# A decoder layer with an expert FFN: the first tile's output projection in three split passes

## The chip, the core and the metric

The kernel runs on one core of a Trainium2 chip. A core has five engines, each with its own queue that runs in order: TensorE (matrix products, PE in the rows), VectorE (DVE), ScalarE (ACT), GpSimd (POOL) and SyncE (SP), and 16 DMA engines. They wait for each other through semaphores only. The metric is the device time of one execution in microseconds, from the first instruction to the end; lower is better.

## What is computed

The reference is one hybrid decoder layer on 256 tokens of width 1024, in float32. The part that matters here is the mixer's output projection, `o @ w_out` of 1024 by 1024:

```python
def hybrid_mixer(h, w_in, b_forget, rel_bias, g_moba_out, g_fox_out, w_out):
    ...
    o_a = moba_attention(hd(qm, N_HEADS_MOBA), hd(km, N_HEADS_MOBA), hd(vm, N_HEADS_MOBA), rel_bias)
    o_b = forgetting_attention(hd(qf, N_HEADS_FOX), hd(kf, N_HEADS_FOX), hd(vf, N_HEADS_FOX),
                               fl + b_forget)
    o = jnp.concatenate([rmsnorm(o_a.reshape(B, S, MOBA_WIDTH), g_moba_out),
                         rmsnorm(o_b.reshape(B, S, FOX_WIDTH), g_fox_out)], axis=-1)
    return o @ w_out
...
    x = x + hybrid_mixer(...)
    x = x + memory_cross_attention(rmsnorm(x), rmsnorm(mem), ...)
    x = x + peer_ffn(rmsnorm(x), ...)     # per token 8 heads x 16 experts: rows of expert_down and expert_up
```

After the mixer come the cross-attention to 256 memory tokens and the expert FFN, which for each token fetches 128 rows of two expert tables.

## The kernel before

The 256 tokens are two tiles of 128 (tile 0 and tile 1). Everything up to the expert FFN is written as one list of steps, `main`, by hand: a step is a tuple such as `("S", t, i)`, `("PT", t, i)`, `("O", t, i)` (scores, transposed probabilities and values of head i of tile t) or `("wout", t, b, part)` (a quarter, two of the eight 128-row chunks, of block b of the output projection). TensorE, VectorE and ScalarE each walk the same list, and each does its own share of a step, so the place of a step in the list is its place in three queues. On VectorE and ScalarE a step in quarters stands where its last quarter stands.

The input projections and the memory's keys and values are products of split numbers: each float32 operand is split into a high part, rounded to the short format float32r, and a low part, the rest; high x high, high x low and low x high are added up in PSUM (`split_product`). The high part of a weight half is a ScalarE cast into `SPARE` (step `high`, L736), the low part a VectorE subtraction in place (step `low`, L976). The output projection is in plain float32 (`product`, L1374).

The attention of tile 0 is woven with the memory's values: eight rounds, p = 0 to 7, of one pair of heads and three or four quarters. After round 4 the first eight heads are normalised and squared (`o_out`, L1044; `o_root`, L667 and L680), after round 7 the other eight. `o_scale` (L1052) multiplies by the root's inverse, `oT` transposes one half on TensorE and VectorE writes it, times the gain, into `HT[0]` (`gained`, L926). Then the projection of tile 0 is woven into the attention of tile 1, tile 1's projection stands behind tile 0's cross-attention, and tile 0's first expert numbers are found by VectorE (`first_head`). GpSimd then issues one indirect DMA for each of 2 x 128 sets of 128 expert rows (L644), VectorE takes dot products of what lands (L1274), ScalarE makes a diagonal of weights and TensorE adds the rows up (L1634).

SyncE's queue issues the weight loads in a written order; each waits until the block that held the slot has been used (`load_block`). `w_out` lies in slots 0 and 1 for both tiles.

## Time and profile before

| | |
|---|---|
| median of 3 runs | 877.69 us (876.02 to 877.87) |
| the profiled execution, its own time | 878.16 us |
| its span, first to last instruction | 876.4 us |
| TensorE busy | 783.6 us, 89% |
| VectorE busy | 558.0 us, 64% |
| ScalarE busy | 437.9 us, 50% |
| GpSimd busy | 249.2 us, 28% |
| DMA | 316.80 MB, mean 362 GB/s |
| mean granted TensorE clock | 0.983 |

The busy shares are means over stages with different limits: up to some 235 us the layer's dense part runs, behind it the expert rows stream in. Clocks and times in the trace are those of the one profiled execution.

### The profile page before, as it was taken

The numbers are of one execution on the slowest core, as the hardware profiler recorded it, in microseconds if no ns is written. First come the engines' busy times: TensorE is split into PE (matmuls) and PEld (weight loads), VectorE is DVE, ScalarE is ACT, GpSimd is POOL, SyncE is SP. The second block draws the span as 40 slices with busy tenths as digits, with TensorE's granted clock in tenths as the row PEclk, the third lists the DMA queues.
The fourth block names the chain that finished last, engine by engine and source line by source line (L and its number), as shares of the span: only waits on it lengthen the run. The fifth ranks groups of instructions, "written<-read, shape, count | busy, mean of one in ns | idle before, by whom it ended". The sixth has DMA issues, their size and how long they took to land.

```text
span 876.4 us, 9609 instructions
## 1 busy us (share of the span) xinstructions
PE 783.6 (89%) x3144; PEld 445.7 (51%) x3144; DVE 558.0 (64%) x1374; ACT 437.9 (50%) x1105; POOL 249.2 (28%) x277
## 2 busy tenths in 40 slices
PE   8999999999999999888898997979787878888776
PEld 8999996895456455444343542544232322323222
DVE  5556443133888767777677658787666766666445
ACT  6447465342264554776545345545455454545344
POOL 1000000000343433434433441533333333343331
PEclk9999999999999999999999999989999999999999
DMA  9956931253899999999999999999999999999995
GB/s 352 417 149 166 424 122 82 72 217 144 318 423 420 402 423 420 421 422 421 421 421 422 420 421 403 418 423 421 420 421 423 421 424 421 423 421 422 421 422 238
DMA packets 44959, 316.80 MB, mean 362 GB/s; under 512 B 5075, under 2 KB 7156, under 8 KB 9972
## 3 DMA queue, kind: packets, MB, share of 16 engines
q0 software_dynamic: 37296, 268.98, 74.1%
q1 hardware_dynamic: 6588, 45.72, 13.2%
q10 hardware_dynamic: 1032, 1.57, 1.3%
q8 instruction: 22, 0.36, 0.2%
q14 instruction: 21, 0.17, 0.0%
HBM read 313.63 MB, written 2.62 MB: 361 GB/s over the span
## 4 chain that ended last, share of the span: by engine, by line
PE 43%; DMA 38%; DVE 8%; ACT 7%; issue 3%; SPq 0%; POOL 0%; POOLq 0%; DVEq 0%; ACTq 0%
DMA weights<-in_expert_rows,expert_idx 21%; PE y L1634 10%; DMA qkvb<-in_expert_rows,expert_idx 8%; PE v_bank L1634 8%; DMA mem_k<-in_expert_rows,expert_idx 7%; PE v_bank L1381 5%; PE v_bank L1374 4%; PE h_psum L1374 4%; PE h_psum L1381 3%; PE a_bank L1381 3%; PE a_bank L1374 2%; DVE weights L1274 2%; DMA spare_row<-in_expert_rows,expert_idx 1%; ACT diag L838 1%; ACT L829 1%
## 5 line engine op out<-in xcount | busy, mean ns | idle before, releaser
L829 ACT ACTIVATE gelu<-dots,stat 128x1 f32<-128x1 f32 x256 | 75.1, 294 | 291.4 <-DVE dots L1274 290.9
L644 POOL DMA_INDIRECT weights<-in_expert_rows,expert_idx x153 | 144.8, 947 | 252.1 <-PE y L1634 106.1
L1634 PE MATMUL v_bank<-weights,diag 128*128 128x512 f32 x316 | 157.9, 634 | 34.6 <-ACT diag L838 34.6
L1634 PE MATMUL y<-weights,diag 128*128 128x512 f32 x296 | 139.1, 606 | 13.8 <-ACT diag L838 13.8
L1274 DVE CUSTOM_DVE_ANT_0 weights<-a_bank,weights 128x1024 f32<-128x1024 f32 x79 | 96.7, 1224 | 63.9 <-DMA weights<-in_expert_rows,expert_idx 63.8
L1634 PEld LDWEIGHTS v_bank<-weights,diag 128*128 128x128 f32 x316 | 57.7, 197 | 130.6 <-ACT diag L838 79.3
L1274 DVE CUSTOM_DVE_ANT_0 weights<-h_psum,weights 128x1024 f32<-128x1024 f32 x74 | 90.5, 1223 | 45.9 <-DMA weights<-in_expert_rows,expert_idx 45.5
L838 ACT ACTIVATE diag<-ident,wgt 128x128 f32<-128x128 f32 x255 | 102.4, 401 | 8.3
L1634 PEld LDWEIGHTS y<-weights,diag 128*128 128x128 f32 x296 | 54.2, 192 | 81.2 <-issue 50.7
L644 POOL DMA_INDIRECT qkvb<-in_expert_rows,expert_idx x61 | 58.2, 954 | 107.7 <-PE v_bank L1634 44.4
L833 ACT ACTIVATE wgt<-gelu,gates 128x1 f32<-128x1 f32 x256 | 75.4, 294 | 8.3
L1634 PE MATMUL v_bank<-qkvb,diag 128*128 128x512 f32 x116 | 56.5, 611 | 10.2 <-ACT diag L838 10.2
L1634 PE MATMUL y<-qkvb,diag 128*128 128x512 f32 x128 | 59.9, 600 | 6.1 <-ACT diag L838 6.1
L976 DVE TENSOR_TENSOR weights_r<-weights,spare_r 128x2048 fp32r<-128x2048 f32 x18 | 41.3, 2292 | 30.2 <-ACT spare_r L736 30.2
L627 POOL DMA_INDIRECT gfin<-in_expert_rows,last_idx x1 | 1.1, 1102 | 198.2 <-PE y L1515 198.2
L1274 DVE CUSTOM_DVE_ANT_0 qkvb<-a_bank,qkvb 128x1024 f32<-128x1024 f32 x30 | 36.7, 1224 | 25.6 <-DMA qkvb<-in_expert_rows,expert_idx 25.5
L1274 DVE CUSTOM_DVE_ANT_0 qkvb<-h_psum,qkvb 128x1024 f32<-128x1024 f32 x32 | 39.1, 1223 | 17.3 <-DMA qkvb<-in_expert_rows,expert_idx 17.1
L736 ACT CAST spare_r<-weights 128x2048 fp32r<-128x2048 f32 x18 | 34.2, 1900 | 27.0 <-PE v_bank L1381 17.5
L1634 PEld LDWEIGHTS v_bank<-qkvb,diag 128*128 128x128 f32 x116 | 20.2, 189 | 44.9 <-ACT diag L838 28.9
L1634 PEld LDWEIGHTS y<-qkvb,diag 128*128 128x128 f32 x128 | 23.0, 190 | 34.9 <-issue 21.5
L644 POOL DMA_INDIRECT spare_row<-in_expert_rows,expert_idx x30 | 28.4, 946 | 39.8 <-PE y L1634 19.4
L1381 PE MATMUL v_bank<-scaled_gffn_r,spare_r 128*128 128x256 f32 x128 | 37.3, 291 | 1.2 <-DVE weights_r L962 1.2
(305 smaller groups left out, 1354.9 us busy)
## 6 DMA issues: line engine op xcount, KB each, us to landing
weights<-in_w_in SPq DMA_DIRECT2D x4, 2048.0 KB, 23.2
weights<-in_w_xk SPq DMA_DIRECT2D x2, 2048.0 KB, 13.8
weights<-in_w_xv SPq DMA_DIRECT2D x2, 2048.0 KB, 15.3
weights<-in_w_out SPq DMA_DIRECT2D x2, 2048.0 KB, 18.3
weights<-in_w_xq SPq DMA_DIRECT2D x2, 2048.0 KB, 7.9
weights<-in_w_xo SPq DMA_DIRECT2D x2, 2048.0 KB, 10.0
weights<-in_expert_rows,expert_idx POOLq DMA_INDIRECT x153, 15.1
weights<-in_w_in SPq DMA_DIRECT2D x2, 1024.0 KB, 12.2
```

What stands on the lines that cost most here:

```text
L627: pool.indirect_dma_start(gfin, None, half_rows, bass.IndirectOffsetOnAxis(ap=last_idx[:, 0:1], axis=0))\
L644: pool.indirect_dma_start(ROWS[buffer(n)], None, expert_rows, bass.IndirectOffsetOnAxis(ap=IDX[:, H % 3, k:k + 1], axis=0))\
L736: act.copy(WH_r[t % 2], half_block(t, W)).then_inc(high_ready, 1)
L829: nc.scalar.activation(gel[:, i:i + 1], dots[:, dot_of(n):dot_of(n) + 1], ACT.Gelu, scale=rms("root_p", n // SPT)).then_inc(gelu_done, 1)
L833: nc.scalar.activation(wgt[:, i:i + 1], gel[:, i:i + 1], ACT.Copy, scale=GATE[:, H % 3, k:k + 1])\
L838: nc.scalar.activation(diag[:, i, :], ident[:, :], ACT.Copy, scale=wgt[:, i:i + 1])\
L976: nc.vector.tensor_tensor(half_block(t, W_r), half_block(t, W), WH_r[t % 2].bitcast(f32), ALU.subtract).then_inc(low_ready, 1)
L1274: nc.vector.tensor_tensor_reduce(out=rows, in0=HP[n // SPT][:, :], in1=rows, scale=1.0, scalar=0.0, op0=ALU.mult, op1=ALU.add, accum_out=d ...
L1374: ins = nc.tensor.matmul(bank[:, lo:lo + n], lhs(k), rhs(k), start=(k == 0), stop=(k == chunks - 1))
L1381: ins = nc.tensor.matmul(bank[:, lo:lo + n], a(k), b(k), start=(begins and k == 0 and p == 0), stop=(ends and k == KC - 1 and p == 2))
L1634: ins = nc.tensor.matmul(YP[t][:, b * BLK:(b + 1) * BLK], diag[:, i, :], ROWS[r][:, D + b * BLK:D + (b + 1) * BLK], start=False, stop=last)
```

## The change

The projection of tile 0 becomes a split product in three passes. Its weights are split in eight pieces of two chunks by one block of 512 columns (`out_split(n)`): `out_high` on ScalarE casts a piece into one of four pages of 1024 columns (the second half of `spare_row`, `gfin`, the second page of `SG`, and `HTpage[1]`), `out_low` on VectorE subtracts in place in the weight slot. Pages are used twice; the second use waits until TensorE has used the first (`out_used`). The evacuation of `oT` of tile 0 writes a high part (`OH_r`, one instruction) and a low part (`OL_r`, four instructions). Since the low parts overwrite `w_out`, and tile 1 still projects in plain float32, SyncE loads both blocks a second time; the load of the gains `gffn` moves behind that, its wait is dropped, and the loads of `w_xq` come before both.

```diff
+    out_parts = [(b, 2 * half + c) for half in range(2) for b in range(2) for c in range(2)]
+
+    def out_split(n):
+        return [("out_high", n, 0), ("out_low", n, 0)]
...
-        main += {4: [("o_out", 0, 0), ("o_root", 0, 0), ("o_scale", 0, 0)],
-                 6: [("oT", 0, 0)]}.get(p, [])
+        main += {4: [("o_out", 0, 0), ("o_root", 0, 0), ("o_scale", 0, 0)] + out_split(0), 5: out_split(1),
+                 6: [("oT", 0, 0)] + out_split(2), 7: out_split(3)}.get(p, [])
     main += late + [("o_out", 0, 1), ("o_root", 0, 1)]
...
-    main += wout[0][:2] + pair("S", 1, 0) + wout[1][:2] + [("o_scale", 0, 1), ("oT", 0, 1)]
-    main += whole_pair(1, 0, wout[0][2:3]) + wout[0][3:] + whole_pair(1, 1, wout[1][2:3]) + wout[1][3:]
+    main += wout[0][:2] + pair("S", 1, 0) + [("o_scale", 0, 1)] + out_split(4) + wout[1][:2] + [("oT", 0, 1)] + out_split(5)
+    main += pair("PT", 1, 0) + pair("S", 1, 1) + out_split(6) + wout[0][2:3] + pair("O", 1, 0) + wout[0][3:] + out_split(7)
+    main += whole_pair(1, 1, wout[1][2:3]) + wout[1][3:]
...
-            sp.wait_ge(*full(("wina", 5, 1)))
-            sp.dma_start(gffn[:, :], A["norm_ffn"][0:1, :].broadcast_to([P, D])).then_inc(ld_gffn, 16)
             load_block("w_xq", 0)
             load_block("w_xq", 1)
+
+
+            for b in range(2):
+                sp.wait_ge(*full(("wout", 0, b)))
+                sp.dma_start(W[:, SLOT[("w_out", b)], :], A["w_out"][b]).then_inc(w_full[SLOT[("w_out", b)]], 16)
+            sp.dma_start(gffn[:, :], A["norm_ffn"][0:1, :].broadcast_to([P, D])).then_inc(ld_gffn, 16)
...
+                elif name == "out_high":
+
+                    b = out_parts[t][0]
+                    act.wait_ge(w_full[SLOT[("w_out", b)]], 16 * NTH[("w_out", b)])
+                    if t >= 4:
+                        act.wait_ge(out_used, t - 3)
+                    elif t >= 2:
+                        act.wait_ge(*full(("wina", 5, 1)))
+                    act.copy(out_pages[t % 4], out_block(t, W)).then_inc(out_high, 1)
...
+                elif name == "out_low":
+                    dve.wait_ge(out_high, t + 1)
+                    nc.vector.tensor_tensor(out_block(t, W_r), out_block(t, W), out_pages[t % 4].bitcast(f32),
+                                            ALU.subtract).then_inc(out_low, 1)
+                elif name == "oT" and t == 0:
+                    src = job(key)
+                    gain = gcol[:, 8 + 4 * i:12 + 4 * i].unsqueeze(2).broadcast_to([P, 4, P])
+                    nc.vector.tensor_tensor(OH_r[:, 4 * i:4 * i + 4, :], src[:, :].rearrange("p (c x) -> p c x", c=4),
+                                            gain, ALU.mult).then_inc(oh_ready, 1)
+                    dve.wait_ge(oh_ready, i + 1)
+                    for c in range(4):
+                        k = 4 * i + c
+                        ins = nc.vector.scalar_tensor_tensor(out=OL_r[:, k, :], in0=src[:, c * P:(c + 1) * P],
+                                                             scalar=gcol[:, 8 + k:9 + k], in1=OH_r[:, k, :].bitcast(f32),
+                                                             op0=ALU.mult, op1=ALU.subtract)
+                    ins.then_inc(v_free, 1)
...
+                    if t == 0:
+                        n = out_parts.index((i, part))
+                        w_low, w_high = out_block(n, W_r), out_pages[n % 4]
+                        if part % 2 == 0:
+                            pe.wait_ge(*freed(("oT", t, part // 2)))
+                        pe.wait_ge(out_low, n + 1)
+                        ins = split_product(bank, 0, BLK, lambda k: OH_r[:, k, :], lambda k: OL_r[:, k, :],
+                                            lambda k: w_high[:, k % 2, :], lambda k: w_low[:, k % 2, :],
+                                            range(2 * part, 2 * part + 2))
+                        if part < 2:
+                            ins.then_inc(out_used, 1)
```

ScalarE's queue from the root of tile 0's first half to the copy of round 6's transposes stood like this before (`stat` is the root, `mem_v` the memory's values, `spare_row` the probabilities and their transposes, `spare_r` the high parts):

```order
L680 ACTIVATE stat<-stat,eps 128x1 [waits sum_done]
L707 ACTIVATE mem_v<-h_psum,stat 128x256 [waits rows_root,m_full]
L707 ACTIVATE mem_v<-h_psum,stat 128x256
L767 COPY spare_row<-a_bank 128x128 [waits a_full] x2
L762 ACT_TABLE_LOAD [waits a_full]
L762 ACTIVATE spare_row,row_sum<-s_sb,neg_max 128x128 [waits v_free]
L762 ACTIVATE spare_row,row_sum<-s_sb,neg_max 128x128 [waits a_full,v_free]
L736 CAST spare_r<-weights 128x2048 [waits m_full,w_full4]
L767 COPY spare_row<-a_bank 128x128 [waits a_full] x2
```

Here the memory's values follow the root at once. ScalarE's queue at the same place now, with the lines of the changed file:

```order
L699 ACTIVATE stat<-stat,eps 128x1 [waits sum_done]
L764 CAST spare_row_r<-weights 128x1024 [waits w_full0]
L726 ACTIVATE mem_v<-h_psum,stat 128x256 [waits rows_root,m_full]
L726 ACTIVATE mem_v<-h_psum,stat 128x256
L795 COPY spare_row<-a_bank 128x128 [waits a_full] x2
L790 ACT_TABLE_LOAD [waits a_full]
L790 ACTIVATE spare_row,row_sum<-s_sb,neg_max 128x128 [waits v_free]
L790 ACTIVATE spare_row,row_sum<-s_sb,neg_max 128x128 [waits a_full,v_free]
L755 CAST spare_r<-weights 128x2048 [waits m_full,w_full4]
L764 CAST gfin_r<-weights 128x1024 [waits w_full0]
L795 COPY spare_row<-a_bank 128x128 [waits a_full] x2
```

The cast into `spare_row_r` has come ahead of the memory's values and of the copies of round 5, the cast into `gfin_r` ahead of the copies of round 6.

VectorE's queue from the maxima of tile 0's last scores (`s_sb,neg_max`) over the first half's `oT` (written to `x_and_h` out of `v_bank`) to the normalisation of the second half (`x_and_h` out of `y`) stood like this before:

```order
L1036 ISA s_sb,neg_max<-v_bank,fox_mask 128x128 [waits p_ready,v_full]
L1036 ISA neg_max 128x1
L926 TENSOR_TENSOR x_and_h<-v_bank,x_and_h 128x512 [waits v_full]
L976 TENSOR_TENSOR weights_r<-weights,spare_r 128x2048 [waits high_ready]
L1042 RECIPROCAL row_inv<-row_sum 128x8 [waits p_ready]
L1044 TENSOR_TENSOR x_and_h<-y,row_inv 128x512 [waits o_full,dve_ch]
```

Here one large subtraction (L976) lies between the transposes and the normalisation. VectorE's queue at that place now:

```order
L1064 ISA s_sb,neg_max<-v_bank,fox_mask 128x128 [waits p_ready,v_full]
L1064 ISA neg_max 128x1
L1088 TENSOR_TENSOR x_and_h_r<-v_bank,x_and_h 128x512 [waits v_full]
L1093 SCALAR_TENSOR_TENSOR scaled_gffn_r<-v_bank,x_and_h,x_and_h_r 128x128 [waits oh_ready]
L1093 SCALAR_TENSOR_TENSOR scaled_gffn_r<-v_bank,x_and_h,x_and_h_r 128x128 x3
L1083 TENSOR_TENSOR weights_r<-weights,scaled_gffn_r 128x1024 [waits out_high]
L1004 TENSOR_TENSOR weights_r<-weights,spare_r 128x2048 [waits high_ready]
L1083 TENSOR_TENSOR weights_r<-weights,x_and_h_r 128x1024 [waits out_high]
L1070 RECIPROCAL row_inv<-row_sum 128x8 [waits p_ready]
L1072 TENSOR_TENSOR x_and_h<-y,row_inv 128x512 [waits o_full,dve_ch]
```

Two subtractions (L1083) have come between the transposes and the normalisation, one on either side of the large subtraction (L1004), and four products (L1093) behind the evacuation.

VectorE's queue from the root's inverse and the scaling of the second half (`x_and_h` by `stat`) to the maxima of tile 1's second pair of heads (`s_sb,neg_max`) stood like this before:

```order
L902 RECIPROCAL stat<-stat 128x1 [waits sq_done]
L1052 TENSOR_SCALAR x_and_h<-x_and_h,stat 128x512 [waits dve_ch]
L926 TENSOR_TENSOR x_and_h<-v_bank,x_and_h 128x512 [waits v_full]
L1036 ISA s_sb,neg_max<-v_bank,qkvb 128x256 [waits p_ready,v_full]
L1036 ISA neg_max 128x1
```

Here the transposes follow the scaling at once. VectorE's queue at that place now:

```order
L930 RECIPROCAL stat<-stat 128x1 [waits sq_done]
L1080 TENSOR_SCALAR x_and_h<-x_and_h,stat 128x512 [waits dve_ch]
L1083 TENSOR_TENSOR weights_r<-weights,spare_row_r 128x1024 [waits out_high]
L1088 TENSOR_TENSOR x_and_h_r<-v_bank,x_and_h 128x512 [waits v_full]
L1093 SCALAR_TENSOR_TENSOR scaled_gffn_r<-v_bank,x_and_h,x_and_h_r 128x128 [waits oh_ready]
L1093 SCALAR_TENSOR_TENSOR scaled_gffn_r<-v_bank,x_and_h,x_and_h_r 128x128 x3
L1083 TENSOR_TENSOR weights_r<-weights,gfin_r 128x1024 [waits out_high]
L1064 ISA s_sb,neg_max<-v_bank,qkvb 128x256 [waits p_ready,v_full]
L1064 ISA neg_max 128x1
```

The evacuation of the second half's transposes now has one subtraction ahead of it and, after its own four products, another behind it.

## Rows read from the trace of the kernel before

**Rows 1.** Busy us of each engine (instructions), PEclk, DMA share, GB/s, by stretch.

```profile
136.60:156.50 19.90, 19.90 (x76) 10.42 (x75) 5.04 (x17) 8.77 (x23) 0.00 (x0) 1.00 0.01 1
156.50:200.00 43.50, 42.06 (x345) 39.23 (x344) 11.66 (x43) 19.17 (x53) 0.00 (x0) 1.00 0.36 146
200.00:233.00 33.00, 32.80 (x107) 16.68 (x106) 20.10 (x72) 7.88 (x15) 6.28 (x6) 1.00 0.56 207
550.00:870.00 320.00, 264.22 (x599) 103.58 (x597) 212.73 (x514) 153.37 (x428) 117.96 (x129) 0.97 1.00 414
```

**Rows 2.** Timeline of GpSimd: start, us, line, [idle before <-releaser].

```profile
221.12 0.94 POOL L644 DMA_INDIRECT qkvb<-in_expert_rows,expert_idx  x1 [18.53 <-DVE expert_idx L1130]
```

**Rows 3.** Chain that ended last: start, us, what, of TensorE's products.

```profile
33.35 25.61 PE v_bank L1381 x216
...
136.73 3.49 PE h_psum L1374 x8
```

**Rows 4.** Groups by shape in the first stage: busy us, mean ns.

```profile
L958 DVE SCALAR_TENSOR_TENSOR x_and_h_r<-x_and_h,scaled_gffn_r 128x256 fp32r<-128x256 f32 x8 | 3.5, 483 | 4.9 <-ACT scaled_gffn_r L718 4.9
...
L967 DVE TENSOR_TENSOR weights_r<-weights,spare_r 128x1024 fp32r<-128x1024 f32 x2 | 2.4, 1222 | 0.2 <-ACT spare_r L724 0.2
...
L724 ACT CAST spare_r<-weights 128x1024 fp32r<-128x1024 f32 x2 | 2.1, 1046 | 0.0
```

**Rows 5.** Timeline of ScalarE, 122 to 142 us.

```profile
122.83 0.43 ACT L767 COPY spare_row<-a_bank 128x128 f32<-128x128 f32 x2
...
131.31 1.89 ACT L736 CAST spare_r<-weights 128x2048 fp32r<-128x2048 f32 x1
...
137.56 0.63 ACT L667 ACTIVATE scaled_gffn<-x_and_h 128x512 f32<-128x512 f32 x1 [0.35 <-DVE x_and_h L1044]
...
141.35 0.51 ACT L762 ACTIVATE spare_row<-s_sb,neg_max 128x256 f32<-128x256 f32 x1 [0.16 <-DVE neg_max L1036]
```

**Rows 6.** Timeline of TensorE, 123 to 220 us.

```profile
123.15 0.66 PE L1515 MATMUL y<-qkvb,spare_row 128*128 128x64 f32 x4 [0.75 <-ACT spare_row L767]
...
136.56 3.65 PE L1374 MATMUL h_psum<-weights,x_and_h 128*128 128x512 f32 x8
...
144.32 0.60 PE L1369 MATMUL v_bank<-ident,x_and_h 128*128 128x128 f32 x4
...
146.33 1.98 PE L1374 MATMUL h_psum<-weights,x_and_h 128*128 128x512 f32 x4
...
157.78 0.60 PE L1369 MATMUL v_bank<-ident,x_and_h 128*128 128x128 f32 x4
...
219.06 14.00 PE L1374 MATMUL v_bank<-weights,x_and_h 128*128 128x512 f32 x32
```

**Rows 7.** Timeline of VectorE, 133 to 146 us.

```profile
133.24 2.29 DVE L976 TENSOR_TENSOR weights_r<-weights,spare_r 128x2048 fp32r<-128x2048 f32 x1 [0.68 <-ACT spare_r L736]
...
136.84 0.69 DVE L1044 TENSOR_TENSOR x_and_h<-y,row_inv 128x512 f32<-128x512 f32 x1 [1.20 <-PE y L1515]
...
144.95 0.69 DVE L926 TENSOR_TENSOR x_and_h<-v_bank,x_and_h 128x512 f32<-128x512 f32 x1 [2.70 <-PE v_bank L1369]
```

**Rows 8.** Busy us, clock and DMA around a wait of TensorE.

```profile
536.00:542.00 6.00, 3.64 (x8) 1.06 (x6) 5.59 (x15) 4.76 (x10) 0.00 (x0) 1.00 1.01 419
542.00:548.00 6.00, 5.67 (x10) 2.42 (x11) 4.98 (x18) 3.13 (x10) 3.75 (x4) 0.72 0.93 351
```

**Rows 9.** Timeline of TensorE after waits, four matmuls each.

```profile
363.82 1.98 PE L1634 MATMUL y<-weights,diag 128*128 128x512 f32 x4 [2.19 <-ACT diag L838]
...
542.33 3.11 PE L1634 MATMUL y<-mem_v,diag 128*128 128x512 f32 x4 [2.19 <-ACT diag L838]
...
575.82 3.78 PE L1634 MATMUL v_bank<-mem_v,diag 128*128 128x512 f32 x4 [4.97 <-ACT diag L838]
...
797.65 3.29 PE L1634 MATMUL v_bank<-weights,diag 128*128 128x512 f32 x5 [2.19 <-ACT diag L838]
```

**Rows 10.** DMA issues: count, KB each, median us to landing.

```profile
weights<-in_w_out SPq DMA_DIRECT2D x2, 2048.0 KB, 18.3
```

More of the change, by code:

```diff
@@ L297, in hybrid_layer @@
         with first:
-            W_r, SPARE_r, QKVB_r, XH_r, SG_r, diag_r = [
+            W_r, SPARE_r, QKVB_r, XH_r, SG_r, diag_r, spare_row_r, gfin_r = [
                 first.enter_context(nc.sbuf_tensor(name + "_r", shape, f32r))
                 for name, shape in (("weights", [P, W_SLOTS, KC * BLK]), ("spare", [P, 4, D]), ("qkvb", [P, 8, D]),
-                                    ("x_and_h", [P, XH_W]), ("scaled_gffn", [P, 2, D]), ("diag", [P, NS, P]))]
+                                    ("x_and_h", [P, XH_W]), ("scaled_gffn", [P, 2, D]), ("diag", [P, NS, P]),
+                                    ("spare_row", [P, 2 * D]), ("gfin", [P, D]))]
         W = sb("weights", [P, W_SLOTS, KC * BLK])
@@ L307, in hybrid_layer @@
         diag = sb("diag", [P, NS, P])
+        spare_row, gfin = sb("spare_row", [P, 2 * D]), sb("gfin", [P, D])[:, :]
         Q, K = [QKVB[:, 2 * i:2 * i + 2, :].rearrange("p a (c t x) -> p (a c) t x", t=T, x=P) for i in range(2)]
@@ L322, in hybrid_layer @@
         Ssb = sb("s_sb", [P, 2, SEQ])
-        spare_row = sb("spare_row", [P, 2 * D])
         both = spare_row[:, 0:D].rearrange("p (a x) -> p a x", a=4)
@@ L397, in hybrid_layer, with out_block @@
               W[:, wslot("w_xq", 0), 0:D].rearrange("p (h x) -> p h x", h=PH)]
-        gfin = sb("gfin", [P, D])[:, :]
+        OH_r, OL_r = [of.rearrange("p (k x) -> p k x", k=KC) for of in (XH_r[:, D:2 * D], SG_r[:, 0, :])]
+        out_pages = [of.rearrange("p (k c) -> p k c", k=2) for of in
+                     (spare_row_r[:, D:2 * D], gfin_r[:, :], SG_r[:, 1, :], XH_r[:, 2 * D + GAINS:3 * D + GAINS])]
+        def out_block(n, of):
+            b, c = out_parts[n]
+            return of[:, wslot("w_out", b), :].rearrange("p (k c) -> p k c", k=KC)[:, 2 * c:2 * c + 2, :]
         spread_of = [XPr[:, w, :] for w in range(2)]
@@ L1524, in step @@
                     if begins:
-                        weights("w_out", i)
+                        if t:
+                            pe.wait_ge(w_full[SLOT[("w_out", i)]], 16 * (NTH[("w_out", i)] + 1))
                         bank_for(key)
-                    for c in quarter(part):
+                    if t == 0:
[9 more added lines that the diff above has]
+                            ins.then_inc(out_used, 1)
+                    for c in quarter(part) if t else []:
                         if c in (0, 2):
```

1 line of the change is left out of this document (added).

## The prediction

> **What bounds the kernel now.** Read first the stretches of the profile [rows 1]. From 550 to 870 us the DMA engines are fully busy at 414 GB/s, fetching one set of expert rows after another (256 in all): this part lasts as long as its bytes, and it begins when the first fetch can be issued. That is the fetch at 221.12, for which GpSimd waited on VectorE's expert numbers [rows 2]. Before it, TensorE is the bound: it is busy for 19.90 of 19.90 us from 136.6 to 156.5, for 42.06 of 43.50 from there to 200 and for 32.80 of 33.00 from 200 to 233, while the DMA share is 0.01 in the first of these [rows 1]. So the end of the kernel moves by what the first fetch moves, and that moves by what TensorE, in front of it, gains or loses. There is hardly any idle time between 158 and 221 in which a delay could vanish: a microsecond lost at 158 is lost at 221, and is lost at the end.
>
> The change works between 120 and 160 us, so the question is what each engine does there.
>
> **What TensorE saves.** The projection of the first tile is 16 products of 512 columns, in eight quarters of two. Four records, one quarter, take half of the 3.49 us that eight take [rows 3], 1.745 us. In three passes a quarter is six matmuls of 512 columns. Their price is not in the trace, but 216 matmuls of the same kind with 256 columns take 25.61 us [rows 3], 118.6 ns each. Upper bound for 512: twice that, 237 ns. Lower bound: 256 columns at 2.4 GHz are 107 ns, so 12 ns are fixed, and if they are paid once a 512-column matmul takes 225 ns; if not at all, 213. I take 225: a quarter is 1.35 us, eight are 10.8 against 14.0, and **3.2 us are saved** (2.6 to 3.7).
>
> The Trainium skill, page "TensorE: Matmul & The Clock Gate", section "Back-to-back issue gap", gives about 131 ns for a sustained stream of 512-column matmuls. By it a quarter would be 0.8 us and the eight would save 7.7. The row above speaks against it: 256 columns already take 118.6.
>
> **What ScalarE and VectorE pay.** Eight casts (high parts) and eight subtractions (low parts) of 128x1024 are new. The same forms stand in the first stage at 1046 and 1222 ns [rows 4]; instructions in a row overlap by about 0.09, so each adds 0.95 and 1.14 us to its queue. The evacuation of each transposed half (0.69 us before) gets four products of 128x128 behind it; the nearest row has 128x256 at 483 ns [rows 4], so I take 0.29 for the first and 0.21 for the others (bounds 0.15 and 0.48), 0.97 with a wait. In all 7.6 us on ScalarE and 11 on VectorE. Both have idle time enough in total, but their queues run in order, and these instructions stand ahead of work that TensorE waits for. I follow that chain.
>
> 1. The first cast stands between the root of the first half's norm and the copies of transposed probabilities at 122.83 [rows 5]. TensorE already waits 0.75 us for these copies at 123.15 [rows 6]. So +0.95, at once and in full, for TensorE and for all behind on ScalarE.
> 2. VectorE's last but one large subtraction waits for a ScalarE cast and moves by that 0.95. Behind it now stands the second new subtraction, 1.14, ahead of the maxima of the last score pair. The exponentials, a copy and the last large cast (131.31) [rows 5] follow these on ScalarE: that cast moves by 2.1, to 133.4, and ends at 135.3. The third new cast runs behind it until 136.35.
> 3. VectorE's third new subtraction waits for that cast, and behind it in the queue stand the last large subtraction (133.24 before), the fourth new one, and the normalisation of the second half (136.84 before, done at 137.53) [rows 7]. Now: 136.4 + 1.14 + 2.2 + 1.14 + 0.9 = 141.8 as its end. **The second half's output is 4.3 us late.**
> 4. ScalarE's sum of squares for it (137.56) starts at 141.85. From there to the next exponentials at 141.35 it took 3.8 us with two table loads, 0.16 of them a wait [rows 5]; the exponentials now start at 145.5 and end at 146.5. TensorE's first four quarters and the score step between them took from 136.56 to 144.32, of which 0.8 are not quarters [rows 6]; now they end at 136.56 + 0.95 + 5.4 + 0.8 = 143.7. What was saved is spent on waiting: 1.2 us for the scaling (the root 2.3 us after 141.85, then 0.7 on VectorE, 144.9), then 1.1 us for the exponentials.
> 5. The fifth cast stands behind the exponentials: until 147.5. The fifth subtraction waits for it: until 148.75. The evacuation of the second half's transposes (144.95 before [rows 7]) stands behind that one: 148.7 + 0.69 + 0.97 = 150.35. The third quarter of the first block needs it, and starts at 150.7 after one score product; before, it started at 146.33 [rows 6]. TensorE stands still for some 3 us here.
> 6. From 146.33 to the transposes at 157.78 [rows 6] there were 11.45 us, 6.98 of them four quarters. With four at 1.35 it is 9.9 us, and later casts and subtractions keep up to within 0.1 us. The transposes come at 150.7 + 9.9 = 160.5: **2.7 us late**.
>
> **The clock.** After waits of TensorE the trace often shows the lower clock. The granted clock was 1.00 from 536 to 542 and 0.72 from 542 to 548 [rows 8]; in that stretch four matmuls that take 1.98 us took 3.11 after a wait of 2.19 us, and 3.78 after one of 4.97 [rows 9]. Not each time: after 2.19 us at 363.82 they took 1.98 [rows 9]. Of ten waits over 2 us from 363.82 to 797.65, seven were followed by 1.2 GHz, both of those over 2.7 among them. From 136.6 to 156.5 the clock is 1.00 now [rows 1]. Step 5 opens a wait of 3 us, with 1.2 and 1.1 shortly before. I expect the fall, and price it by these rows at 0 to 1.9 us of TensorE's time, 1.1 taken, since part of the slow time may fall into the wait itself.
>
> **The loads.** The second load of the weights waits for the last quarter of each block, and for nothing later; issued at about 156 and 160 us it lands 18.3 us later if it is as slow as the first [rows 10], by 180. The second tile reads it at 219.06 [rows 6]. The copy of the gains is queued behind it and is wanted only for the first dots after that. DMA is idle then. Cost nothing, with some 40 us to spare; without that cover each 2 MB would cost its landing time. SP's next wait is for the last half of the memory values, which comes later than both, so nothing else is held up.
>
> **The sum.** 2.7 + 1.1 = 3.8 us. The profiled execution took 878.16, 0.47 above the median of the runs, 877.69. So 878.16 + 3.8 = 882.0 for such an execution, and **881.5 us** as the median.
>
> **The rivals.** This kernel's measurement can tell about 0.2%, 1.75 us, from no change: 875.9 to 879.4.
> - Waits as reckoned, but the clock holds: 877.69 + 2.7 = 880.4. For it: the clock is 1.00 in all three stretches before 233 [rows 1], and three of ten waits had no effect. Chance 0.22.
> - The waits are hidden and TensorE's saving arrives: only step 1 is paid, 877.69 - 3.2 + 0.95 = 875.4, faster. It is decided in step 2: if the third cast ends before VectorE has evacuated the first half's transposes (about 134.4), neither the normalisation nor what follows is late. For it: ScalarE is busy only 8.77 of 19.90 us [rows 1]. Against it: the cast is 2 us too late by my chain, and step 5 stands even then. Chance 0.09.
> - Half of it: the normalisation is late by 2 us rather than 4, the queue at step 5 costs 2 us; loss and saving cancel, 878.0, same. Chance 0.13.
> - The passes take far less than 225 ns, so that TensorE makes up in step 6 what it lost: at 60% of that, step 6 is 7.7 us, the delay 0.5 and the time 878.2, same. Against it stand the 118.6 ns for 256 columns [rows 3]. Chance 0.02. This is what the Trainium skill's 131 ns would come to.
> - My chance for the reckoned case, 881.5, is 0.48; the rest, 0.06, goes to a longer spell at 1.2 GHz, above 884.
>
> Slower: 0.48 + 0.22 + 0.06 = 0.76, and 0.01 from the edge of the half case. Leaving out the faster case, the lower part of the half case and the long spell gives 8 in 10 from 877.4 to 884.0. Inside the likeliest case the bounds (passes 213 to 237 ns, products 0.15 to 0.48, clock 0 to 1.9) give 880.0 to 883.5.
>
> **What would show it.** Right: the copies at 122.83 about 0.95 later; the second normalisation near 141; TensorE idle before the second half's transposes, before the first transposes of the second tile's probabilities, and for some 3 us before the third quarter; a granted clock under 1.00 between 147 and 156; the first fetch near 225, and the stretch behind it as long as before. Wrong: a quarter far from 1.35 us, a third cast that ends by 134, casts or subtractions shorter in this place than in the first stage, or a wait at 219 for the second load.

## The result and the profile after

The changed kernel takes **883.25 us** (median of 5 runs, 881.90 to 884.48) against 877.69. It is slower by 5.6 us in the medians; the ratio of the runs is 1.0067, 95% interval 1.0056 to 1.0079. The profiled execution took 882.83 us, its span is 881.0, its mean granted clock 0.981.

First the stretches of the changed kernel, with the columns of [rows 1]: busy us of TensorE, its weight loads, VectorE, ScalarE and GpSimd (instructions), then the granted clock, the DMA share and GB/s.

```profile
125.00:127.00 2.00, 2.00 (x11) 2.00 (x11) 0.00 (x0) 2.00 (x5) 0.00 (x0) 0.50 0.00 0
...
148.00:150.00 2.00, 0.00 (x0) 0.00 (x0) 1.96 (x6) 0.75 (x3) 0.00 (x0) 0.50 0.00 0
150.00:154.00 4.00, 3.65 (x8) 2.52 (x9) 2.25 (x8) 2.20 (x6) 0.00 (x0) 0.50 0.01 4
...
136.60:156.50 19.90, 16.29 (x72) 11.74 (x72) 11.76 (x23) 11.85 (x22) 0.00 (x0) 0.83 0.05 19
156.50:200.00 43.50, 42.67 (x337) 39.13 (x336) 12.29 (x43) 17.89 (x50) 0.00 (x0) 1.00 0.64 254
200.00:233.00 33.00, 32.18 (x131) 18.69 (x131) 16.79 (x59) 9.11 (x22) 5.23 (x5) 1.00 0.40 149
550.00:870.00 320.00, 261.82 (x600) 102.45 (x599) 213.52 (x519) 150.92 (x423) 122.56 (x132) 0.98 1.01 419
```

From 136.6 to 156.5 TensorE was busy for all 19.90 us before [rows 1]; now it is busy for 16.29, and part of that at half clock. The clock falls to 0.50, the lower of its two levels (1.2 GHz), twice: shortly before 125 us and at 148 us. (Below, the first is called the fall at 125 us.) Behind 156.5 the engines' picture is the old one; the larger DMA share up to 200 us holds the second load of the weights, and the expert rows still stream at full DMA. GpSimd's first fetch, at 221.12 before [rows 2]:

```profile
226.60 0.94 POOL L663 DMA_INDIRECT qkvb<-in_expert_rows,expert_idx  x1 [18.52 <-DVE expert_idx L1174]
```

It comes 5.48 us later on the clock of the two traces; from it to the end of the span there are 654.4 us, 655.3 before. So the loss arises ahead of the first fetch, as the prediction had it. The start of a program differs from one execution to the next: TensorE's transposes of round 4's probabilities begin at 111.81 here and began at 112.59 before, and nothing of the change lies ahead of them. Counted from there the first fetch is 114.79 - 108.53 = **6.26 us late**. This count is used below; it frees a single trace of what differs at its start.

The places that the prediction named. ScalarE's timeline (start, us, what) of the changed kernel, the new cast ahead of the copies of round 5:

```profile
121.34 1.03 ACT L764 CAST spare_row_r<-weights 128x1024 fp32r<-128x1024 f32 x1
122.27 0.83 ACT L726 ACTIVATE mem_v<-h_psum,stat 128x256 f32<-128x256 f32 x2
123.00 0.43 ACT L795 COPY spare_row<-a_bank 128x128 f32<-128x128 f32 x2
```

VectorE's, with the third and the fourth new subtraction ahead of the second half's normalisation (L1072), and the fifth ahead of the evacuation of its transposes (L1088):

```profile
135.48 1.23 DVE L1083 TENSOR_TENSOR weights_r<-weights,scaled_gffn_r 128x1024 fp32r<-128x1024 f32 x1 [0.45 <-ACT scaled_gffn_r L764]
...
139.50 1.22 DVE L1083 TENSOR_TENSOR weights_r<-weights,x_and_h_r 128x1024 fp32r<-128x1024 f32 x1 [0.59 <-ACT x_and_h_r L764]
...
140.87 0.69 DVE L1072 TENSOR_TENSOR x_and_h<-y,row_inv 128x512 f32<-128x512 f32 x1
...
147.30 1.23 DVE L1083 TENSOR_TENSOR weights_r<-weights,spare_row_r 128x1024 fp32r<-128x1024 f32 x1 [2.65 <-ACT spare_row_r L764]
148.45 0.68 DVE L1088 TENSOR_TENSOR x_and_h_r<-v_bank,x_and_h 128x512 fp32r<-128x512 f32 x1
149.17 1.13 DVE L1093 SCALAR_TENSOR_TENSOR scaled_gffn_r<-v_bank,x_and_h,x_and_h_r 128x128 fp32r<-128x128 f32 x4
```

And TensorE's, which waits for both places:

```profile
123.31 0.66 PE L1559 MATMUL y<-qkvb,spare_row 128*128 128x64 f32 x4 [1.72 <-ACT spare_row L795]
...
145.90 0.93 PE L1550 MATMUL a_bank<-ident,spare_row 128*128 128x128 f32 x4 [0.53 <-ACT spare_row L790]
146.76 0.70 PE L1531 MATMUL v_bank<-qkvb 64*128 64x256 f32 x2
150.35 1.22 PE L1531 MATMUL v_bank<-qkvb 64*128 64x256 f32 x2 [2.89 <-DVE scaled_gffn_r L1093]
151.50 0.79 PE L1425 MATMUL h_psum<-spare_row_r,x_and_h_r 128*128 128x512 f32 x1
...
163.23 0.60 PE L1413 MATMUL v_bank<-ident,x_and_h 128*128 128x128 f32 x4
...
224.53 1.98 PE L1418 MATMUL v_bank<-weights,x_and_h 128*128 128x512 f32 x4
```

The wait for round 5's copies has grown from 0.75 [rows 6] to 1.72 us. The score product at 150.35 waits 2.89 us for VectorE's products and then takes 1.22 us, where two such took 0.7 at 146.76. The third quarter, at 146.33 before [rows 6], starts at 151.50. The second tile's projection at 224.53 waits for nothing: the second load is there.

### The profile page after: what moved, and what is told of

It reads as the page before. It is cut to its first block, busy times and chain, and to the rows that moved or that the text cites. A ratio compares the mean times of both kernels' runs of the same rounds, so it can differ in the third digit from the quotient of the medians.

```text
span 881.0 us, 9675 instructions
## 1 busy us (share of the span) xinstructions
PE 781.6 (89%) x3160; PEld 448.5 (51%) x3160; DVE 569.5 (65%) x1390; ACT 445.2 (51%) x1113; POOL 250.5 (28%) x277
## 4 chain that ended last, share of the span: by engine, by line
PE 44%; DMA 37%; ACT 7%; DVE 6%; issue 3%; POOL 1%; SPq 0%; POOLq 0%; DVEq 0%; ACTq 0%
DMA weights<-in_expert_rows,expert_idx 22%; PE y L1690 12%; DMA qkvb<-in_expert_rows,expert_idx 8%; PE v_bank L1690 5%; PE v_bank L1425 5%; PE h_psum L1425 5%; PE v_bank L1418 4%; DMA mem_k<-in_expert_rows,expert_idx 4%; PE a_bank L1418 4%; DMA mem_v<-in_expert_rows,expert_idx 3%; PE a_bank L1425 3%; PE h_psum L1418 2%; DVE weights L1318 2%; ACT diag L866 1%; ACT wgt L861 1%
## 5 line engine op out<-in xcount | busy, mean ns | idle before, releaser
L1690 PE MATMUL v_bank<-weights,diag 128*128 128x512 f32 x316 | 155.1, 623 | 37.7 <-ACT diag L866 37.7
L1004 DVE TENSOR_TENSOR weights_r<-weights,spare_r 128x2048 fp32r<-128x2048 f32 x18 | 41.3, 2292 | 29.0 <-ACT spare_r L755 29.0
```

What stands on the lines that cost most here:

```text
L1004: nc.vector.tensor_tensor(half_block(t, W_r), half_block(t, W), WH_r[t % 2].bitcast(f32), ALU.subtract).then_inc(low_ready, 1)
L1690: ins = nc.tensor.matmul(YP[t][:, b * BLK:(b + 1) * BLK], diag[:, i, :], ROWS[r][:, D + b * BLK:D + (b + 1) * BLK], start=False, stop=last)
```

## The experiments

The table gives each kernel's median with the number of runs, its ratio to the kernel before, timed beside it (877.08 to 877.69), and, of its one profile, TensorE's wait for round 5's copies, the granted clock from 125 to 127 us, and how late the first fetch is, counted as above. In e_best and e_place new casts do stand ahead of that mark, but it comes 26.18 us behind round 0's transposes in both, as before (26.17). The kernels were timed in several groups, so times of different rows are best compared by what each is above the kernel before beside it.

| kernel | us (runs) | ratio, 95% | wait | clock | first fetch |
|---|---|---|---|---|---|
| changed | 883.25 (5) | 1.0067, 1.0056 to 1.0079 | 1.72 | 0.50 | +6.26 |
| e_again | 882.24 (5) | 1.0059, 1.0046 to 1.0073 | 1.71 | 0.50 | +6.43 |
| e_first | 883.13 (5) | 1.0065, 1.0052 to 1.0079 | 0.75 | 1.00 | +5.73 |
| e_lows | 880.19 (5) | 1.0035, 1.0021 to 1.0048 | 1.72 | 1.00 | +3.75 |
| e_fifth | 880.12 (5) | 1.0036, 1.0022 to 1.0050 | 1.71 | 1.00 | +3.73 |
| e_fill | 880.63 (5) | 1.0040, 1.0026 to 1.0054 | 0.20 | 1.00 | +3.53 |
| e_onecast | 878.26 (11) | 1.0010, 1.0001 to 1.0019 | 1.70 | 0.50 | +2.09 |
| e_load | 877.34 (11) | 1.0000, 0.9991 to 1.0009 | 0.77 | 1.00 | +0.03 |
| e_best | 878.08 (11) | 1.0017, 1.0008 to 1.0026 | none | 1.00 | +0.78 |
| e_place | 874.12 (5) | 0.9963, 0.9950 to 0.9977 | 0.78 | 1.00 | -2.29 |

In the edits, `out_high(n)` and `out_low(n)` are the two halves of `out_split(n)`, each a step of its own; their definitions are left out.

**The second and the third step undone: e_lows.**

```diff
-                 6: [("oT", 0, 0)] + out_split(2), 7: out_split(3)}.get(p, [])
-    main += late + [("o_out", 0, 1), ("o_root", 0, 1)]
+                 6: [("oT", 0, 0)] + out_high(2), 7: out_high(3)}.get(p, [])
+    main += late + [("o_out", 0, 1), ("o_root", 0, 1)] + out_low(2) + out_low(3)
```

> The changed kernel with the third and fourth subtraction moved behind the normalisation and squaring of the second half; the casts stay. Theory (step 3 of the prediction, the normalisation waits behind the third subtraction): the normalisation, at 140.87 now, comes some 2 us earlier and the third quarter at about 148 instead of 151.5; 880 to 881.3, and down to 879.3 if the clock then stays at 1.00 from 148 to 155 us. Rival (the second half is late for the work ahead of it, first cast and the last large cast, not for these subtractions): 882.7 to 883.5.

VectorE's normalisation of the second half and TensorE ahead of the third quarter (two views):

```profile
136.73 0.69 DVE L1078 TENSOR_TENSOR x_and_h<-y,row_inv 128x512 f32<-128x512 f32 x1
```

```profile
146.69 1.22 PE L1537 MATMUL v_bank<-qkvb 64*128 64x256 f32 x2 [2.04 <-DVE scaled_gffn_r L1099]
147.84 0.79 PE L1431 MATMUL h_psum<-spare_row_r,x_and_h_r 128*128 128x512 f32 x1
```

The normalisation is some 4 us earlier than in the changed kernel, where the theory had 2, and the third quarter some 3.5; TensorE still waits 2.04 us just before, and the clock falls all the same (0.52 from 146 to 152 us). The median, 880.19, is within the theory's range, with the clock's second fall still in it: 3.1 us above the kernel before, where the changed kernel stood 5.6 and, repeated, 5.05 above. In the profiles the first fetch is 2.5 us earlier; 0.7 of these are the first fall, which this profile does not show (below).

**The fifth step undone: e_fifth.**

```diff
-    main += late + [("o_out", 0, 1), ("o_root", 0, 1)]
+    main += late + [("o_out", 0, 1), ("o_root", 0, 1)] + out_high(4)
...
-    main += wout[0][:2] + pair("S", 1, 0) + [("o_scale", 0, 1)] + out_split(4) + wout[1][:2] + [("oT", 0, 1)] + out_split(5)
+    main += wout[0][:2] + pair("S", 1, 0) + [("o_scale", 0, 1)] + out_low(4) + wout[1][:2] + [("oT", 0, 1)] + out_split(5)
```

> The changed kernel with the fifth cast moved from behind tile 1's first exponentials to the place right behind the squares of the second half's norm; the fifth subtraction stays ahead of the second evacuation of transposes. Theory (step 5, the evacuation waits for a subtraction that waits for a cast behind the exponentials): the subtraction no longer waits 2.65 us for the cast, the third quarter starts some 1.5 to 2.5 us earlier, and the time is 880 to 881.8, about 881, with a shorter spell or none at granted clock 0.50 between 148 and 155 us. Rival (the cast only moves its 0.95 us from one place of ScalarE's queue to another, in front of the exponentials that TensorE waits for): 882.7 to 884.

The fifth subtraction on VectorE, and TensorE's timeline at the place (two views):

```profile
144.00 1.23 DVE L1089 TENSOR_TENSOR weights_r<-weights,spare_row_r 128x1024 fp32r<-128x1024 f32 x1 [0.25 <-ACT spare_row_r L770]
```

```profile
143.80 0.65 PE L1419 MATMUL v_bank<-ident,x_and_h 128*128 128x128 f32 x4 [0.60 <-DVE x_and_h L1086]
145.93 1.18 PE L1556 MATMUL a_bank<-ident,spare_row 128*128 128x128 f32 x4 [1.48 <-ACT spare_row L796]
147.04 1.23 PE L1537 MATMUL v_bank<-qkvb 64*128 64x256 f32 x4
```

The long wait is gone, but the cast now stands ahead of the exponentials, and the wait for those is 1.48 instead of 0.53 us, the cast's 0.95. The clock falls here too (0.50 from 146 to 152). Theory and rival hold in part: the subtraction waits 0.25 us for its cast instead of 2.65, and 0.95 is paid elsewhere; 880.12 is within the theory's range. Either undoing gives 2 to 3 us of the loss, and each leaves 3.0 to 3.1: the two steps are links of one chain.

**The first step undone: e_first.**

```diff
-        main += {4: [("o_out", 0, 0), ("o_root", 0, 0), ("o_scale", 0, 0)] + out_split(0), 5: out_split(1),
+        main += {4: [("o_out", 0, 0), ("o_root", 0, 0), ("o_scale", 0, 0)], 5: out_split(0) + out_split(1),
```

> The changed kernel with the first cast and subtraction moved behind round 5's copies, next to the second ones; the same work, only its place differs. Theory (the queue, with the clock behind it): in the changed kernel TensorE waited 1.72 us for round 5's copies and was granted 0.50 from 125 to 127 us; with the cast gone from in front of the copies that wait returns to about 0.75 us, the clock stays at 1.00 from 123 to 130, and the time falls by 1.0 (queue) to 2.5 us (queue and clock), part of it given back because the two casts now stand together: 881 to 882.3, about 881.5. Rival (the first fall of the clock has another cause than the longer wait): the clock falls all the same, and the time is 882.3 to 883.3. Rival (the critical chain is that of the third and fifth cast alone): no change, 883.2.

The wait is 0.75 again and the clock stays up from 123 to 130 us, and yet nothing is won: my theory's 881.5 was wrong, the rival's "no change" right. VectorE's timeline of this kernel shows where the cast went:

```profile
129.25 1.22 DVE L1089 TENSOR_TENSOR weights_r<-weights,spare_row_r 128x1024 fp32r<-128x1024 f32 x1
130.39 1.22 DVE L1089 TENSOR_TENSOR weights_r<-weights,gfin_r 128x1024 fp32r<-128x1024 f32 x1
131.52 0.28 DVE L1070 CUSTOM_DVE_ANT_0 s_sb<-v_bank,fox_mask 128x128 f32<-128x128 f32 x1
```

Both subtractions now stand ahead of the maxima of round 7's scores, on which exponentials, the last large cast, the third new cast and the normalisation hang. TensorE waits 0.71 us for these maxima at 131.96, and the normalisation comes at 140.93, 21.37 us behind round 5's transposes, where without a fall of the clock it was 21.19 (e_fifth). A piece moved by one round stays in the same chain.

**The clock: e_fill.** Seven small matmuls fill the wait for round 5's copies, three of 512 columns the wait before the score product (behind a wait for `o_raw`, so that the bank is free); none of their results is read.

```diff
-        main += late + now[2:3] + pair("O", 0, p) + now[3:]
+        main += late + now[2:3] + ([("fill", 0, 7)] if p == 5 else []) + pair("O", 0, p) + now[3:]
...
-    main += pair("PT", 1, 0) + pair("S", 1, 1) + out_split(6) + wout[0][2:3] + pair("O", 1, 0) + wout[0][3:] + out_split(7)
+    main += pair("PT", 1, 0) + [("fill", 1, 3)] + pair("S", 1, 1) + out_split(6) + wout[0][2:3] + pair("O", 1, 0) + wout[0][3:] + out_split(7)
...
```

> The changed kernel with ten matmuls added that compute nothing that is read: seven small ones in TensorE's wait for round 5's copies, three of 512 columns in its wait before tile 1's second score product. They shorten the two idle times and leave every other queue as it is. Theory (the two falls of the granted clock, 0.50 from 125 to 127 and from 148 to 154 us, follow from TensorE's idle time, and cost about 1.5 and 1.9 us): with the idle time filled the clock stays higher and the time falls by 1.5 to 3.4 us, to 880 to 881.7. Rival (the clock falls for another reason, or its cost was hidden in the waits): 882.7 to 884, the added matmuls costing up to 0.7 us.

The stretches of this kernel, columns as above, and its TensorE where the second wait was:

```profile
123.00:130.00 7.00, 6.74 (x57) 6.40 (x58) 3.61 (x7) 5.44 (x11) 0.00 (x0) 1.00 0.00 0
136.60:148.00 11.40, 10.20 (x43) 6.37 (x42) 6.96 (x12) 8.60 (x16) 0.00 (x0) 1.00 0.01 2
148.00:156.00 8.00, 7.68 (x38) 5.27 (x37) 6.21 (x14) 3.63 (x8) 0.00 (x0) 1.00 0.15 29
```

```profile
145.78 2.74 PE L1579 MATMUL y<-qkvb,ident 128*128 128x512 f32 x6
148.45 0.70 PE L1537 MATMUL v_bank<-qkvb 64*128 64x256 f32 x2
149.46 0.70 PE L1537 MATMUL v_bank<-qkvb 64*128 64x256 f32 x2 [0.32 <-DVE scaled_gffn_r L1099]
150.09 0.50 PE L1431 MATMUL h_psum<-spare_row_r,x_and_h_r 128*128 128x512 f32 x1
...
160.30 0.60 PE L1419 MATMUL v_bank<-ident,x_and_h 128*128 128x128 f32 x4
```

VectorE's and ScalarE's queues are those of the changed kernel, and the third quarter still waits for them. What differs besides the filled waits is the clock: 1.00 throughout, and 880.63 is what the theory gave. The first fetch is 3.53 us late instead of 6.26. The medians differ by 2.6 us; above the kernel before beside each, the changed kernel stands 5.6 and 5.05 and this one 3.55, so 1.5 to 2.0. So of the loss in the profile **3.5 us are queues and 2.7 are clock**. Of the 2.7, 2.05 arise between the normalisation and the transposes of step 6 (140.87 to 163.23 in the changed kernel, 22.36 us; 139.99 to 160.30 here, 20.31): the second fall. The other 0.7 stand ahead of it: the first. That the matmuls in the first wait are what kept the clock up there is not shown by this one profile, since two other profiles have the whole wait and no fall (below).

**The changed kernel again, and one cast alone: e_again, e_onecast.** The second is the kernel before with one unread cast:

```diff
-        main += {4: [("o_out", 0, 0), ("o_root", 0, 0), ("o_scale", 0, 0)],
+        main += {4: [("o_out", 0, 0), ("o_root", 0, 0), ("o_scale", 0, 0), ("extra", 0, 0)],
...
+                elif name == "extra":
+                    act.wait_ge(w_full[SLOT[("w_out", 0)]], 16 * NTH[("w_out", 0)])
+                    act.copy(spare_row[:, D:2 * D], W[:, SLOT[("w_out", 0)], 0:D])
```

> The changed kernel unaltered, profiled and timed once more beside the others. It asks which of the two falls of the granted clock belong to it. If the fall at 125 us follows from TensorE's wait of 1.72 us there, the profile shows 0.50 again between 124 and 128 us and the first fetch 6.2 to 6.3 us later than in the kernel before, counted from round 5's transposes. If it is chance, as its absence after the same wait in the profiles with the subtractions or the fifth cast moved suggests, the clock stays at 1.00 there and the first fetch is 4.7 to 5.4 us late; the second fall, 148 to 154 us, shows in both cases. Time 882.0 to 883.5.

> The kernel before with one cast of 128x1024 added on ScalarE at the place of the changed kernel's first cast; its result is read by nobody. Theory (step 1 of the prediction: a queue that TensorE waits for passes the whole cast on): round 5's copies and TensorE behind them come 0.95 us later, the first fetch 0.8 to 1.0 us later, the time is 877.1 + 0.95 = 878.0, a ratio of 1.0009 to 1.0013. If TensorE's longer wait, 1.7 us, brings the granted clock down as it did in the changed kernel's first profile, 879.3 to 879.7; the wait of 1.72 us stood in three more profiles without a fall, so the first is likelier. Rival (later slack takes the cast up): 877.1, ratio 1.000.

One cast at that place makes the kernel slower, by 1.07 us in the medians (0.1 to 1.7 by the interval): nothing behind it takes it up, though ScalarE was busy for only half of the span. e_again shows the first fall again. But it is not the wait alone that brings it. The same wait, 1.70 to 1.72 us, stands in five profiles; the clock is 0.50 from 125 to 127 us in three (changed, e_again, e_onecast) and 1.00 in two (e_lows, e_fifth; two, not three as expected for e_onecast), which run the changed kernel's instructions unaltered up to there. Wait and stretch of e_lows:

```profile
123.05 0.32 PE L1565 MATMUL y<-qkvb,spare_row 128*128 128x64 f32 x1 [1.72 <-ACT spare_row L801]
```

```profile
123.00:130.00 7.00, 6.79 (x57) 6.45 (x58) 3.60 (x7) 5.39 (x10) 0.00 (x0) 1.00 0.01 2
```

In e_onecast's profile the fall costs 2.09 - 0.95 = 1.1 us. The profiled execution, with the fall in it, took 878.19 us, no more than the median, 878.26, so the times do not tell in how many executions the clock falls; that stays open.

**The second load alone: e_load.** The kernel before with SyncE's part of the change and TensorE's wait for it.

```diff
-            sp.wait_ge(*full(("wina", 5, 1)))
-            sp.dma_start(gffn[:, :], A["norm_ffn"][0:1, :].broadcast_to([P, D])).then_inc(ld_gffn, 16)
             load_block("w_xq", 0)
             load_block("w_xq", 1)
+            for b in range(2):
+                sp.wait_ge(*full(("wout", 0, b)))
+                sp.dma_start(W[:, SLOT[("w_out", b)], :], A["w_out"][b]).then_inc(w_full[SLOT[("w_out", b)]], 16)
+            sp.dma_start(gffn[:, :], A["norm_ffn"][0:1, :].broadcast_to([P, D])).then_inc(ld_gffn, 16)
...
+                        if t:
+                            pe.wait_ge(w_full[SLOT[("w_out", i)]], 16 * (NTH[("w_out", i)] + 1))
                         weights("w_out", i)
```

> The kernel before with the second load of both blocks of the output weights alone, issued at the changed kernel's place and waited for by the second tile's projection; no splitting. Theory (the load is hidden and collides with nothing): 877.1, ratio 0.999 to 1.001, and no wait of TensorE ahead of the second tile's projection near 219 us. Rival (it delays the cross-attention's weights or the gains, which stand behind it in SyncE's queue): TensorE waits for a load between 160 and 220 us, and the time rises by that, up to 10 us for the 4 MB at some 400 GB/s.

Ratio 1.0000, and the first fetch 0.03 us from its old place: 4 MB more cost nothing here.

**Other places: e_best, e_place.** e_best casts and subtracts the first two pieces right behind round 2.

```diff
-        main += {4: [("o_out", 0, 0), ("o_root", 0, 0), ("o_scale", 0, 0)] + out_split(0), 5: out_split(1),
-                 6: [("oT", 0, 0)] + out_split(2), 7: out_split(3)}.get(p, [])
-    main += late + [("o_out", 0, 1), ("o_root", 0, 1)]
+        main += {2: out_split(0) + out_split(1), 4: out_high(2) + out_high(3) + [("o_out", 0, 0), ("o_root", 0, 0)] + out_low(2) + out_low(3) + [("o_scale", 0, 0)],
+                 6: [("oT", 0, 0)]}.get(p, [])
+    main += late + [("o_out", 0, 1), ("o_root", 0, 1)] + out_high(4)
...
-    main += wout[0][:2] + pair("S", 1, 0) + [("o_scale", 0, 1)] + out_split(4) + wout[1][:2] + [("oT", 0, 1)] + out_split(5)
+    main += wout[0][:2] + pair("S", 1, 0) + [("o_scale", 0, 1)] + out_low(4) + wout[1][:2] + [("oT", 0, 1)] + out_split(5)
```

> The changed kernel with its casts and subtractions placed where the engines' queues have room: the first two pieces behind round 2, the third and fourth casts ahead of the first half's normalisation and root, their subtractions between root and scaling, the fifth cast right behind the second half's squares. The work is the same. Theory (the split passes are worth 14.0 - 11.3 = 2.7 us to TensorE, and only the places of the casts lost it): the second half's normalisation stands no later than in the kernel before, the third quarter waits under 1 us, the clock stays at 1.00 from 123 to 160 us, and the time is 1.5 to 2.5 us under the kernel before, 874.6 to 875.6, ratio 0.997 to 0.9985. Rival (ScalarE and VectorE have no room for 18 us wherever the pieces stand): the wait moves to another place, 877 to 880.

878.08, the rival. VectorE, TensorE and the clock of this kernel (three views):

```profile
105.85 1.23 DVE L1089 TENSOR_TENSOR weights_r<-weights,spare_row_r 128x1024 fp32r<-128x1024 f32 x1 [1.87 <-ACT spare_row_r L770]
106.99 1.22 DVE L1089 TENSOR_TENSOR weights_r<-weights,gfin_r 128x1024 fp32r<-128x1024 f32 x1
...
108.73 0.28 DVE L1070 CUSTOM_DVE_ANT_0 s_sb<-v_bank,fox_mask 128x128 f32<-128x128 f32 x1
```

```profile
114.19 0.36 PE L1431 MATMUL h_psum<-spare_r,weights_r 128*128 128x256 f32 x1 [1.82 <-DVE weights_r L1010]
```

```profile
115.00:118.00 3.00, 3.00 (x19) 3.00 (x18) 0.47 (x3) 3.00 (x6) 0.00 (x0) 0.59 0.99 426
```

The same mistake one stage earlier: the subtractions, late because the first load of the weights had only just landed (their first cast waits 3.12 us for it, until 104.77), stand ahead of maxima, TensorE waits 1.82 us, and the clock falls. From round 5's transposes on, this kernel gains 2.6 us; it had lost 3.4 before. So in e_place the first four subtractions stand behind maxima, and their casts behind a large cast, where the rows of before show the queue idle until the next arrival (two views):

```profile
116.72 2.29 DVE L976 TENSOR_TENSOR weights_r<-weights,spare_r 128x2048 fp32r<-128x2048 f32 x1 [2.53 <-ACT spare_r L736]
```

```profile
112.90 0.43 ACT L767 COPY spare_row<-a_bank 128x128 f32<-128x128 f32 x2 [2.05 <-PE a_bank L1506]
```

Besides, the fifth cast stands right behind the second half's root, and TensorE transposes the second half one quarter earlier; what each of these moves is worth was not measured by itself.

```diff
         main += now[:2] + pair("PT", 0, p) + pair("S", 0, p + 1)
+        main += {4: out_low(0) + out_low(1), 5: out_low(2) + out_low(3)}.get(p, [])
...
+        main += {3: out_high(0) + out_high(1), 4: out_high(2) + out_high(3) + [("o_out", 0, 0), ("o_root", 0, 0), ("o_scale", 0, 0)],
+                 6: [("oT", 0, 0)]}.get(p, [])
+    main += late + [("o_out", 0, 1), ("o_root", 0, 1)] + out_high(4)
...
+    main += wout[0][:2] + pair("S", 1, 0) + [("o_scale", 0, 1)] + out_low(4) + wout[1][:1] + [("oT", 0, 1)] + wout[1][1:2] + out_split(5)
```

> The changed kernel with the pieces placed by the idle times of the trace of before: first two casts behind round 3's large cast, their subtractions behind round 4's maxima; third and fourth cast behind round 4's large cast, their subtractions behind round 5's maxima; fifth cast right behind the second half's root, and the second half's transposes one quarter earlier on TensorE. The placement tried before had put the first two subtractions ahead of round 3's maxima, and TensorE waited 1.82 us for them at 114.19, with the granted clock at 0.50 from 116 to 118. Theory (the gain of the passes is there, 14.0 - 11.3 = 2.7 us, and any place in which no maximum, copy or normalisation stands behind a cast keeps it): clock 1.00 from 105 to 160 us, waits of TensorE at most 0.8 us, first fetch 1.8 to 2.7 us earlier than before counted from the same start, time 874.5 to 875.5, ratio 0.997 to 0.998. Rival (the queues are full and the wait only moves once more): 877 to 879.

**874.12 us**, ratio 0.9963, a little under the theory's range: 3.1 us under the kernel before, timed beside it, and 8 to 9 under the changed one, with the same work. Its stretches:

```profile
110.00:123.00 13.00, 12.22 (x106) 11.54 (x105) 10.27 (x18) 10.81 (x20) 0.00 (x0) 1.00 0.45 161
123.00:136.00 13.00, 12.85 (x109) 12.41 (x109) 8.63 (x15) 8.01 (x19) 0.00 (x0) 1.00 0.44 163
136.00:158.00 22.00, 21.17 (x122) 16.72 (x121) 12.16 (x28) 14.64 (x30) 0.00 (x0) 1.00 0.41 153
```

VectorE is busy for 10.27 and ScalarE for 10.81 of 13 us in the first stretch, with two new subtractions and three new casts in it, and nobody waits for them: TensorE waits 0.78 us for round 5's copies, as before the change, 0.15 at 128.61, also as before, and for no engine from 129 to 156 us. The clock is 1.00.

## Why the prediction was right in its sign and short in its size

The forecast was 881.5, slower by 3.8 us; the median is 883.25, slower by 5.6, inside the range and near the upper end of the likeliest case's own (880.0 to 883.5). The mechanism is the one foreseen: casts and subtractions in queues ahead of work that TensorE waits for. On the clock of the trace of before (0.78 us added to the changed kernel's times, the difference of their starts):

- **Step 1**, 0.95 for the cast: right. The copies start at 123.78 against 122.83, and in e_onecast TensorE's products behind them come 0.93 later, counted from round 4's transposes.
- **Steps 2 and 3**, third cast done at 136.35 and the second normalisation at 141.8: measured 136.2 and 142.3, and 141.7 in e_fifth, whose clock did not fall at 125 us. Right.
- **Step 4**, exponentials done at 146.5: 147.0. The waits behind it came out as at most 0.3 (no record of the profile shows one) and 0.53 us instead of 1.2 and 1.1, since TensorE itself came later, from the fall at 125 us and from slower quarters.
- **Step 5**, TensorE standing still for some 3 us before the third quarter: it waits 2.89 us. Right. The quarter starts at 152.3 and not 150.7, as the normalisation was 0.7 later through the first fall than without it (in the rows above, VectorE waits 0.59 us at 139.50 for a cast, which e_fill's does not), and half of the score product stands behind the wait: 0.35 was reckoned, it is 0.63 at full clock (e_fill) and 1.15 at half.
- **Step 6**, 2.7 us late before the clock is counted: 3.5 in e_fill. Of the 0.8 between, 0.4 stand ahead of the third quarter: it starts there at 151.1 on the clock of before (150.09 and the 1.00 between the starts) and not 150.7, mostly for the score product of step 5. From it to the transposes at 160.30 it takes 10.21 us and not 9.9, as the passes save less. That term was too large: in e_place, where nothing waits, the way from the first quarter to the transposes (135.43 to 154.34) takes 18.91 us, and took 21.22 before (136.56 to 157.78 [rows 6]): the eight quarters save **2.3 us**, not 3.2, and less than the bound of 2.6. In the changed kernel what the first four fail to save mostly disappears in the waits of step 4. The price of a 512-column matmul was at its upper bound, 0.235 us from start to start, and the first of a group takes 0.33 until the next starts, so that a quarter is 1.51 and the eight are some 12.0, not 10.8. The eight in plain float32 were some 14.3 by the same count, not 14.0. The rows of e_place:

```profile
135.43 0.48 PE L1432 MATMUL h_psum<-spare_row_r,x_and_h_r 128*128 128x512 f32 x1
...
144.12 0.50 PE L1432 MATMUL h_psum<-spare_row_r,x_and_h_r 128*128 128x512 f32 x1
144.45 0.40 PE L1432 MATMUL h_psum<-weights_r,x_and_h_r 128*128 128x512 f32 x1
144.69 0.39 PE L1432 MATMUL h_psum<-spare_row_r,scaled_gffn_r 128*128 128x512 f32 x1
...
145.63 1.00 PE L1566 MATMUL y<-qkvb,spare_row 128*128 128x64 f32 x8
...
154.34 0.60 PE L1420 MATMUL v_bank<-ident,x_and_h 128*128 128x128 f32 x4
```

  The Trainium skill's 131 ns (page "TensorE: Matmul & The Clock Gate", section "Back-to-back issue gap") for a sustained stream of 512-column matmuls is not seen here: 0.235 us from start to start is 1.8 times that.
- **The clock**, 0 to 1.9, 1.1 taken: 2.05 for the fall that was foreseen, at its place, and 0.7 for one that was not. This is the larger miss. The rows after waits [rows 9] gave the upper bound, 1.9, well; taking the middle was wrong. Part of the slow time did fall into the wait, as reckoned (0.50 from 148 to 150 us with TensorE idle), but the clock stayed down until shortly before 155, so that some 4.5 us of work behind the wait ran slow as well. The fall at 125 us was left out: step 1 lengthens a wait to 1.7 us, and the prediction weighed only waits above 2.
- **The loads**, nothing: right (e_load).

2.7 + 0.8 (score product and passes) + 2.05 + 0.7 is the 6.3 us of the profile. The medians differ by less, 5.6 and, repeated, 5.05; why stays open. The stretch behind the first fetch differs by about as much between the profiles of the two kernels, 654.4 and 655.3 us.

Of the rivals, "the clock holds" at 880.4 comes near to e_fill's 880.63, in part by luck: above the kernel before beside it e_fill stands 3.55 us, not 2.7. "The waits are hidden" did not happen in the changed kernel; e_place brings it about by other places, 3.1 us faster where 2.3 was reckoned.

## What to carry to other kernels

An instruction that is moved to an engine with idle time is free only behind the last thing in that queue that the critical engine waits for; read the idle stretches of the queue and what ends them, and put new work right behind maxima, copies and normalisations, and ahead of the next ones only as much as fits the idle stretch (e_place: two casts in 2.05 us, and the copies behind them still wait for TensorE). Moving a piece by one step within the same chain can gain nothing (e_first); look for the place where no one waits for the result soon. Count a wait that you open on TensorE twice, once for itself and once for the clock, with the whole price of the slow rows.
